# Last sums of the output projection in the attention's banks, a copy at the joint moved up, and sums of the activations for two pairs of chunks in one operation

## What is computed

```python
def _swiglu(x, w_gate, w_up, w_down):
    return (jax.nn.silu(x @ w_gate) * (x @ w_up)) @ w_down

def _layer(x, ...):
    x = _layer_norm(ALPHA * x + 0.5 * _swiglu(x, ffn1_w_gate, ffn1_w_up, ffn1_w_down), ln1_g, ln1_b)
    h = x @ w_in
    xp, q, k, v, xq, gates = jnp.split(h, SPLITS, axis=-1)
    ...   # pooling branch, attention over a window of 128, cross-attention into 256 memory tokens
    merged = (g[:, :, 0] * (y_pool @ w_br_pool) + g[:, :, 1] * (y_swa @ w_br_swa) + g[:, :, 2] * (y_x @ w_br_cross))
    x = _layer_norm(ALPHA * x + merged @ w_o, ln2_g, ln2_b)
    x = _layer_norm(ALPHA * x + 0.5 * _swiglu(x, ffn2_w_gate, ffn2_w_up, ffn2_w_down), ln3_g, ln3_b)
    return x, new_k, new_v, new_pool
```

## Time and profile before

| what | value |
|---|---|
| median of three runs | 2475.97 us (2474.82 to 2476.84) |
| the profiled execution | 2475.46 us, its span 2472.5 us |
| TensorE, matmuls | busy 2406.2 us, 97% of the span |
| TensorE, loading of weights | 2341.8 us, 95% |
| VectorE | 1622.5 us, 66% |
| ScalarE | 1221.0 us, 49% |
| GpSimd | 623.5 us, 25% |
| mean granted clock of TensorE | 0.988 of full speed |

### The profile page before, as it was taken

The page is one execution under the profiler, slowest core; times in us unless marked ns, Lnnn a source line. Parts: engine busy times, 40 slices in busy tenths (PEclk is TensorE's granted clock), DMA queues, the critical chain, the costliest instruction groups (busy, mean ns, idle before and its releaser), DMA issues.

```text
span 2472.5 us, 45123 instructions
## 1 busy us (share of the span) xinstructions
PE 2406.2 (97%) x17595; PEld 2341.8 (95%) x17595; DVE 1622.5 (66%) x2744; ACT 1221.0 (49%) x2472; POOL 623.5 (25%) x576
## 2 busy tenths in 40 slices
PE   8999999999999899999999999999999998999997
PEld 8999999899999899999999999989999998999997
DVE  4877776635344587777677777664453457877775
ACT  5555655334322465655565656553443225655654
POOL 1233334120000223333423333341100002333333
PEclk9999999989999999999999999999999999999999
DMA  6222233221122212222213222333112231232231
GB/s 229 93 95 95 95 103 123 77 75 50 61 85 86 86 65 91 89 99 96 93 60 107 93 103 78 112 105 109 43 57 69 86 103 51 73 105 97 84 106 56
DMA packets 54178, 221.29 MB, mean 89 GB/s; under 512 B 15856, under 2 KB 18800, under 8 KB 40880
## 3 DMA queue, kind: packets, MB, share of 16 engines
q1 hardware_dynamic: 53968, 218.41, 26.0%
HBM read 213.58 MB, written 6.04 MB: 89 GB/s over the span
## 4 chain that ended last, share of the span: by engine, by line
PE 79%; DVE 12%; ACT 5%; DVEq 2%; issue 1%; POOL 1%; DMA 0%; ACTq 0%; SPq 0%; POOLq 0%
PE pair L1943 12%; PE pair L1945 11%; PE pair L1944 11%; PE pair L1786 9%; PE pair L1790 9%; PE pair L1788 9%; PE S L1943 2%; PE S L1945 2%; PE S L1944 2%; DVE htl L1202 2%; DVE TP L1122 1%; PE S L2057 1%; ACT hth L743 1%; PE TP L2117 1%; PE S L1897 1%
## 5 line engine op out<-in xcount | busy, mean ns | idle before, releaser
L1943 PE MATMUL pair<-xth,hiA 128*128 128x288 f32 x1216 | 358.6, 295 | 0.4
L1944 PE MATMUL pair<-xtl,hiA 128*128 128x288 f32 x1216 | 358.8, 295 | 0.0
L1945 PE MATMUL pair<-xth,loA 128*128 128x288 f32 x1216 | 358.4, 295 | 0.0
L695 ACT ACTIVATE hiA<-TP 128x512 fp32r<-128x512 f32 (+1 forms) x372 | 194.0, 555 | 205.0 <-DVE TP L1127 125.0
L1691 POOL TENSOR_TENSOR loB<-rawB,hiB 128x512 fp32r<-128x512 f32 (+1 forms) x128 | 161.1, 1259 | 493.6 <-ACT hiB L695 493.5
L1113 DVE TENSOR_TENSOR loA<-TP,hiA 128x512 fp32r<-128x512 f32 (+1 forms) x372 | 235.7, 634 | 17.0 <-ACT hiA L695 14.2
L1108 DVE TENSOR_TENSOR loA<-rawA,hiA 128x1024 fp32r<-128x1024 f32 x96 | 119.1, 1242 | 181.9 <-ACT hiA L682 181.2
L1943 PEld LDWEIGHTS pair<-xth,hiA 128*128 128x128 f32 x1216 | 228.0, 188 | 1.1 <-DVE loA L1113 1.1
L1691 POOL TENSOR_TENSOR loB<-rawA,hiB 128x512 fp32r<-128x512 f32 (+1 forms) x120 | 143.3, 1194 | 340.1 <-ACT hiB L695 340.1
L1945 PEld LDWEIGHTS pair<-xth,loA 128*128 128x128 f32 x1216 | 228.7, 188 | 0.0
L1944 PEld LDWEIGHTS pair<-xtl,hiA 128*128 128x128 f32 x1216 | 228.3, 188 | 0.0
(11 more groups left out here) (388 smaller groups left out, 7046.5 us busy)
## 6 DMA issues: line engine op xcount, KB each, us to landing
rawA<-in_wblk SPq DMA_DIRECT2D x104, 512.0 KB, 3.5
rawA<-in_wg SPq DMA_DIRECT2D x44, 1024.0 KB, 4.8
rawB<-in_wg SPq DMA_DIRECT2D x44, 1024.0 KB, 4.7
rawB<-in_wd SPq DMA_DIRECT2D x24, 768.0 KB, 4.1
rawA<-in_wd SPq DMA_DIRECT2D x24, 768.0 KB, 4.4
rawA<-in_wt_d SPq DMA_DIRECT2D x4, 1024.0 KB, 4.8
rawB<-in_wt_d SPq DMA_DIRECT2D x4, 1024.0 KB, 4.7
mcs<-in_mks SPq DMA_DIRECT2D x2, 2048.0 KB, 11.9
```

What stands on the lines that cost most here:

```text
L695: nc.scalar.activation(slot((hiA, hiB), prod, n), src, ACT.Copy).then_inc(f_hi, 1)
L1943: nc.tensor.matmul(bank, wt_hi, xt[0], start=start, stop=False, skip_group_check=True)
L1944: nc.tensor.matmul(bank, wt_hi, xt[1], start=False, stop=False, skip_group_check=True)
L1945: last = nc.tensor.matmul(bank, wt_lo, xt[0], start=False, stop=i == n - 1, skip_group_check=True)
```

## The change

Six edits are made at once.

1. **Start.** The memory tokens come in four transfers of 256 KB; the first weight is transferred behind the first of them, the second behind the fourth. ScalarE rounds and VectorE takes rests in four parts in the same way, with the first two weights behind the first and the third part, and TensorE waits for each two chunks.
2. **Transposes of v.** They move behind one more block of the input's projection.
3. **First block of the pooling's stage.** The scores and transposes that stood behind chunk 4 of the block stand behind chunk 6 (for i = 0 alone).
4. **Sums of x.** Two pairs of chunks are summed by one operation (2 x 288 columns). On ScalarE the rounding of the first sums moves behind the quarters q0 and q1 of g = 2; on VectorE the order in the head is another.
5. **Joint.** ScalarE's copy of u3 at u = HEADS moves ahead of the rounding of the hidden values; VectorE's c22 moves behind the first sums of the next unit.
6. **Banks of the output projection.** m = 6 and 7 lie in S and TP for both halves, so that the second half's blocks wait until VectorE has read the first half's (`half_added`), and the wait at the head's first blocks (g = 0) becomes one at the blocks of g = 1, for m = 4 and 5. VectorE takes the residual of m = 4 ahead of the reciprocal, 5 and 6 inside the scaling, and 7 behind it. In fb = 1 and 3 TensorE issues the second half's mean behind chunk 2 of `block(1, 0, 0)` and the variance behind chunk 5 of `block(1, 1, 0)`.

```diff
-            return pair[m % 2][:, 0, 0:TH] if h else (S, TP)[m % 2][:, 1, 0:TH]
+            return (S, TP)[m % 2][:, 1, 0:TH]
...
-            for s in range(2):
-                sp.dma_start(mem[:, 4 * s:4 * s + 4, :], mem0[:, 4 * s:4 * s + 4, :]).then_inc(mem_in[s], 16)
-                sp.dma_start(raw[:, s, :], wblk[s]).then_inc(raw_in[s], 16)
+            for i in range(4):
+                sp.dma_start(mem[:, 2 * i:2 * i + 2, :], mem0[:, 2 * i:2 * i + 2, :]).then_inc(mem_in[i], 16)
+                if i in (0, 3):
+                    sp.dma_start(raw[:, i // 3, :], wblk[i // 3]).then_inc(raw_in[i // 3], 16)
...
-                round_sums(fb, 0)
                 silu(0, 1)
                 fill_head(fb, 2, 0)
                 fill_head(fb, 2, 1)
+                round_sums(fb, 0)
                 round_sums(fb, 1)
...
                     if u == HEADS:
+                        copy_u3(u)
                         round_hidden(fb, 1, 0)
...
-                b12, b21, b22 = x[:, 2 * i, TH:T], x[:, 2 * i + 1, 0:TH], x[:, 2 * i + 1, TH:T]
-                t1, t3, t2, t4 = (tf[:, i % 2, j, :] for j in range(4))
+                even, odd = slice(4 * k, 4 * k + 4, 2), slice(4 * k + 1, 4 * k + 4, 2)
+                b12, b21, b22 = x[:, even, TH:T], x[:, odd, 0:TH], x[:, odd, TH:T]
+                t1, t3, t2, t4 = (tf[:, :, j, :] for j in range(4))
...
                 sums_of_x(fb, 0)
-                sums_of_x(fb, 1)
-                rest_of_sums(fb, 0)
                 rest_of_quarter(fb, 0)
                 rest_of_quarter(fb, 1)
-                sums_of_x(fb, 2)
+                rest_of_sums(fb, 0)
                 head_hidden(fb, 0, 1)
+                rest_of_sums(fb, 1)
+                sums_of_x(fb, 1)
                 rest_of_quarter(fb, 2)
                 rest_of_quarter(fb, 3)
-                rest_of_sums(fb, 1)
-                sums_of_x(fb, 3)
                 rest_of_sums(fb, 2)
...
                     if more:
                         first_sums(fb, u + 1)
+                    if u == HEADS:
+                        sum_c22(u)
...
+                else:
+                    residual(4, 1)
                 reciprocal(l, n, 0)
...
                     if n == 1 and c in (1, 4):
-                        residual(4 + c // 4, 1)
+                        residual(5 + c // 4, 1)
...
-                    residual(6, 1)
                     residual(7, 1)
...
-                    elif f == 1 and g == 0:
-                        pe.wait_ge(pair_free[w], n_use(fb // 2, Q_WO + 3) + 2)
+                    elif f == 1 and g == 1:
+                        pe.wait_ge(pair_free[w], n_use(fb // 2, Q_WO + 2) + 2)
...
-                        if fb and (g, w, h, c) == (1, 0, 0, 5):
+                        if n == 1 and (g, w, h, c) == (1, 0, 0, 2):
+                            mean(l, n, 1)
+                        if fb and (g, w, h, c) == ((1, 1, 0, 5) if n == 1 else (1, 0, 0, 5)):
                             variance(l, n, 1)
...
-                    if fb and h == 0:
+                    if n == 2 and h == 0:
                         mean(l, n, 1)
...
+                project(l, pq(l, Q_IN + 3), 0, n_use(l, Q_IN + 3))
                 pe.wait_ge(pair_free[1], n_use(l, Q_IN + 2) + 2)
                 pe.wait_ge(t_free, t_count(l, "v") + 1)
...
-                project(l, pq(l, Q_IN + 3), 0, n_use(l, Q_IN + 3))
                 project(l, pq(l, Q_IN + 3), 1, n_use(l, Q_IN + 3))
...
-                        project(l, pq(l, Q_IN + 4), i, n_use(l, Q_IN + 4), between)
+                        project(l, pq(l, Q_IN + 4), i, n_use(l, Q_IN + 4), between, 6 if i == 0 else 4)
...
-                            pe.wait_ge(half_added, l * 4 + m - 5)
+                            pe.wait_ge(half_added, l * 4 + m - 3)
```

More of the change, by code:

```diff
@@ L314, in build @@
         cst_in, x_in, par_in = sem("cst_in"), sem("x_in"), sem("par_in")
-        mem_in = [sem("mem_in0"), sem("mem_in1")]
+        mem_in = [sem(f"mem_in{i}") for i in range(4)]
         raw_in = [sem("raw_in0"), sem("raw_in1")]
@@ L746, in _ @@
             nc.scalar.activation(small[:, 60:61], small[:, 61:62], ACT.Copy)
-            for s in range(2):
-                act.wait_ge(mem_in[s], 16)
-                cs = slice(4 * s, 4 * s + 4)
+            for i in range(4):
+                act.wait_ge(mem_in[i], 16)
+                cs = slice(2 * i, 2 * i + 2)
                 nc.scalar.activation(memh[:, cs, :], mem[:, cs, :], ACT.Copy).then_inc(mem_hi, 1)
-                round_w(0, s)
+                if i in (0, 2):
+                    round_w(0, i // 2)
             for s in range(2):
@@ L839, in fill_next, with copy_u3 @@
                             fill(fb, u + 1, prod)
-                    if old:
-                        act.wait_ge(f_done, done(fb, u - 1, "P7"))
-                        nc.scalar.activation(u3[:, :], al[(u - 1) % 2], ACT.Copy).then_inc(al_act, 1)
+                    def copy_u3(v):
+                        act.wait_ge(f_done, done(fb, v, "P7"))
+                        nc.scalar.activation(u3[:, :], al[v % 2], ACT.Copy).then_inc(al_act, 1)
+                    if old and u > HEADS + 1:
+                        copy_u3(u - 1)
                     if on and u > HEADS:
@@ L1140, in sums_of_x @@
                 else:
[L1141 to L1142 removed]
+                    dve.wait_ge(xf_full, xf_full_count((fb - 1) // 2, (fb - 1) % 2 + 1, 1, 4 * k + 3))
+                if k > 0:
                     dve.drain()
[L1144 removed]
+                nc.vector.tensor_tensor(t1, b12, x[:, even, 0:TH], ALU.subtract)
                 nc.vector.tensor_tensor(t3, b12, b22, ALU.add)
@@ L1159, in _ @@
             nc.vector.memset(small[:, 60:62], 1.0).then_inc(small_set, 1)
-            for s in range(2):
-                cs = slice(4 * s, 4 * s + 4)
-                dve.wait_ge(mem_hi, s + 1)
+            for i in range(4):
+                cs = slice(2 * i, 2 * i + 2)
+                dve.wait_ge(mem_hi, i + 1)
                 nc.vector.tensor_tensor(meml[:, cs, :], mem[:, cs, :], memh[:, cs, :].bitcast(F32), ALU.subtract).then_inc(mem_ready, 1)
-                rest_w(0, s)
+                if i in (0, 2):
+                    rest_w(0, i // 2)
             for i in range(1, PAIR_MEM):
@@ L1269, in ffn, with sum_c22 @@
                     r, r_old = u % 2, (u - 1) % 2
-                    if g_old:
-                        dve.wait_ge(al_act, 2 * g_count(fb, u - 1))
+                    def sum_c22(v):
+                        dve.wait_ge(al_act, 2 * g_count(fb, v))
                         dve.drain()
-                        nc.vector.tensor_tensor(c22[:, :], u3[:, :], de[r_old], ALU.add).then_inc(de_read, 1)
+                        nc.vector.tensor_tensor(c22[:, :], u3[:, :], de[v % 2], ALU.add).then_inc(de_read, 1)
+                    if g_old and u > HEADS + 1:
+                        sum_c22(u - 1)
                     if d_old:
@@ L1806, in begin, with project @@
                     pe.wait_ge(pair_free[s], u + 1)
-            def project(l, qq, s, u, halfway=None):
+            def project(l, qq, s, u, meanwhile=None, after=4):
                 begin(qq, s, u)
                 for c in range(KC):
-                    if c == KC // 2 and halfway:
-                        halfway()
+                    if c == after and meanwhile:
+                        meanwhile()
                     last = mm3(lambda h: pair[s][:, h, 0:TH], wt(s, c), (xs(xh, c), xs(xl, c)), c, KC)
```

8 lines of the change are left out of this document (4 added, 4 removed).

## The result

The changed kernel takes 2484.85 us (median of seven runs, 2477.70 to 2485.94), the kernel before 2474.82 beside it (2472.83 to 2477.68): a ratio of 1.0032, interval 1.0021 to 1.0044. It is slower by 0.3% (0.4% by the two medians), where 2475.7 and no change were forecast, and it lies 1.9 us above the range of 2467 to 2483.

The account below looks back on a forecast made before the run. TensorE, busy 2406.2 of 2472.5 us, was taken to bound the kernel. From 2475.46 us, terms of -10.6 (joint, attention, start, sums of x) and +10.8 (head) gave 2475.7 us, no change; range 2467 to 2483.

Parts of the forecast that it names:

- The joint: Four equal TensorE waits of 1.6 us for u3's copy go when it moves ahead of a rounding: gain 6.6 us.
- if the joint's wait comes back under another name: Sign, looked for in the profile after, that the forecast is wrong about the four joint waits being gone.
- at nothing: VectorE's earlier c22 at the joint costs nothing, since TensorE asks for P5 only 3.2 us later; otherwise 0.45 per joint.
- The attention: Waits of the transposes of v (1.8 us) and of attention probabilities (2.3 us) go: gains.
- The head: Behind the output projection: 5.69 wait removed, but new waits before up block and second half; loss 5.4 us a layer, 10.8 both.
- the clock, 2.8 in a layer: Head's two new idle times: one clock fall charged in full plus 0.5, 2.8 us a layer; bounds nothing to 4.6.
- the second idle time: Head, ahead of the second half: 4.0 us idle, clock charged only 0.5 because TensorE then waits for x anyway.
- that rule: Skill's rule that each burst starts cold: both head idle times paid in full, 14.4 us for both layers, sum 2479.3.
- The sums of x: Wider VectorE sums make the third unit's q2 and q3 late, 0 to 1.0 us per head: cost 0.5 in all.
- The start: Program's start: 256 KB of mem ahead of the first weights, so they come up to 0.7 us earlier; gain 0.4.
- The slower one: Rival: clock falls in the head's first new idle time and stays down; 10.4 us a layer, 2485.7 us; chance 0.18.
- The first rival: Head pays as its first part promises, second half 5.6 us earlier in each layer: 2453.7 us; chance 0.11.

Follow-up runs that it names:

- jointonly: The fifth edit (joint: u3's copy and c22) alone on the kernel before: 2476.54 us, ratio 1.0006 to the kernel before.
- Joint2: The changed kernel with u3's copy and c22 also moved ahead in the unit behind the joint: 2477.77 us, ratio 1.0009 to the kernel before.
- late22: The changed kernel with c22 of the joint back at its old place, u3's copy kept early: 2481.78 us, ratio 1.0025 to the kernel before.
- nof: The changed kernel with its sixth edit (banks, residuals, mean and variance) undone, the other five kept: 2470.55 us, ratio 0.9982 to the kernel before.
- attn: The kernel before with the second and third edits alone (transposes of v, first pooling block): 2469.46 us, ratio 0.9975 to the kernel before.
- before2: The kernel before once more, no edit, for a profile of another execution: 2476.67 us, ratio 1.0003.
- again: The changed kernel once more, no edit, for a profile of another execution: median 2484.33 us, ratio 1.0036 to the kernel before; profiled execution 2485.26.
- oldmean: The changed kernel with the second half's mean and variance at their old places, new banks kept: 2463.24 us, ratio 0.9947 to the kernel before.
- nojoint: The changed kernel with its fifth edit (u3's copy and c22 at the joint) undone: 2480.26 us, ratio 1.0018 to the kernel before.

## Why the prediction was wrong, step by step

**The joint is the step that failed.** "Gain: 6.0 + 4 x 0.16 = 6.6 us" measured 0.15 us of loss in the changed kernel, and 1.6 of loss for the edit alone (jointonly). Two things were missing. First, the sum stopped at the wait removed: what is late next was asked in the head and not here. The unit behind has the same two steps on ScalarE and VectorE, behind a rounding of 1.41 and rests of 1.66, and the hidden sums on which these hang end only 0.3 us earlier than before (VectorE's at 911.40 instead of 911.69), though VectorE comes into the joint 0.7 earlier (its operation on S and rawA starts at 900.13 instead of 900.82). An earlier copy in the joint does not bring them forward. Joint2 shows it: with that unit's two steps moved as well, the gain is there (6.2 us between the joints of the two kernels). So the prediction's own sign, "if the joint's wait comes back under another name", came true. Second, c22 was costed "at nothing, without that cover 0.45 in each of four joints", and the cover was looked for on TensorE alone. It was VectorE that lost it: before, c22 ran while VectorE waited for ScalarE's roundings; ahead of the rests it is on the chain, and each joint lost 0.4 (late22 gives back 1.7 in four).

**The attention** was right in its mechanism (both waits gone, none in their place) and near in its size: 4.1 forecast, 6.2 measured alone, 5.5 and 9.0 in the two profiles. What the profiles have beyond 4.1 is the clock. In layer 0 before runs at 0.50 for 20.4 us; nof, with the edits and the same 20.4, gains 2.2. In layer 1, where before has 17.1, the six traces with the edits and the same 17.1 gain 1.6 to 2.4. With 13.7 in layer 0 the profiled execution gains 5.3, with 23.9 attn gains 0.4; before2 shows such differences without any edit. Whether the edits shorten the stretches at 0.50 on the average stays open.

**The head** was right in each step: the fifth chunk's wait for x (1.68), the mean at 845.87 for 845.37, q3 7.3 us behind it, the second half late by both waits (3.54 with 0.51 for 3.7 with 0.9, and 3.58 for 4.0). Its size was 10.8 and is 12.4 in the profiled execution and 15.8 in that of a usual time. The term that was too small is the clock, 2.8 in a layer: the second idle time, charged 0.5, brought a fall of its own (864 to 866 above), and in layer 1 of the slower one there were three. In the five traces with these waits a head costs more the longer TensorE runs at 0.50 in it: 4.9 us with 6.8 at 0.50, 5.2 to 6.2 with 10.3, 7.4 and 7.5 with 13.7, 8.4 with 17.1. The Trainium skill, "TensorE: Matmul & The Clock Gate", section "HAM oscillation — how this bites in real kernels", says that waits between short bursts of matmuls drop the clock anew for each burst; by that rule the prediction had 14.4 for both layers. The traces agree with it: in those five a fall stands at each of the two long waits of each head (2.8 to 3.6 us), and none stands in the heads of oldmean, which does not have these waits. They also show what the prediction had no row for: in again (layer 1) and joint2 (both layers) a third fall stands behind the shorter waits of 0.4 and 1.5 ahead of them.

**The sums of x** cost 0.4 in each head behind the mixing where TensorE keeps its old pace (nof: +0.40 and +0.43), 0.8 for the 0.5 forecast; and they gave something that was not forecast, 0.7, 0.2 and 0.7 in the joints of the three later half steps, where VectorE comes earlier (nojoint; that this is the fourth edit is inferred, since no run has it alone). **The start** cannot be settled: from -1.6 to +1.5 in ten traces with the edit, -0.8 to +0.7 in three others without it.

**The sum.** In the execution of a usual time the joint missed by 6.75 and the head by 5.0; the attention (-1.4), the start (-0.3), the third unit (-1.1) and the rest (+1.5, whose cause is open) give 10.4 together, for a measured 9.6 (2485.26 - 2475.7; 0.3 more comes behind the last matmul, and less time lies around its span, 1.9 us instead of 3.0).

**The rivals.** The slower one has nearly the time measured, 2485.7, but not by its mechanism: the clock came back between the waits, and the joint made up the rest. (Its sum passes 2480.9 from a loss of 8.0 a layer on, not 7.8.) The first rival's price for the head, 5.6 a layer, is near what oldmean measured (5.0 and 4.85): the banks are worth what their first part promised once the mean does not follow a wait for weights.

## What to carry to other kernels

A wait that is taken away moves the engine that waited forward, and the next stage of the same pattern then meets its own chain; book the gain only after asking, for every stage that repeats the steps, when its last input comes by an order that has not changed. A step that looks free because its engine is idle there is not free at another place of the same engine's order. And when a block of banks is freed, leave the head of the longest chain (here the mean) where it can be issued first: the same banks cost 13.8 us with mean and variance moved behind, and gave 9.9 us in the two heads with both at their old places.

## What the runs showed of the hardware

Executions of one kernel differ by up to 10.5 us (before2: 2470.62 to 2481.15). Two of the kernel before were profiled; they have the same long waits, and differ where TensorE is busy for the whole of a window (4.00 of 4.00 us at 1730 to 1742) and yet runs at 0.50, in stretches whose place and length change from one execution to the other: the stage takes 1.5 us less in layer 0 and 2.4 more in layer 1. A profile of one execution can so lie 7 us from the median of its kernel, as the first one of the changed kernel did.
